# Projecting the first two weight chunks abreast in a hybrid decoder block

## The reference, cut to what matters

```
h = rmsnorm(x, norm_g)                 # x: 1 x 512 x 1024, float32
proj = jnp.einsum('bsd,de->bse', h, w_in)
(lru_u, lru_z, ...) = jnp.split(proj, ...)
xc = conv_b + sum(u_pad[:, k:k + seq] * conv_w[k] for k in range(4))   # lru_u, causal width 4
r = sigmoid(xc @ wa + ba);  i = sigmoid(xc @ wx + bx)                  # per block of 64 channels
```

## Time and profile before

| what | us |
|---|---|
| median of three runs | 414.31 |
| the profiled execution, its own time | 414.59 |
| its span in the profile | 412.8 |
| TensorE busy with matmuls | 405.2 |
| VectorE busy | 283.8 |
| ScalarE busy | 253.0 |

### The profile page before, as it was taken

The page is one execution under the profiler, slowest core; times in us unless marked ns, Lnnn a source line. Parts: engine busy times, 40 slices in busy tenths (PEclk is TensorE's granted clock), DMA queues, the critical chain, the costliest instruction groups (busy, mean ns, idle before and its releaser), DMA issues.

```text
span 412.8 us, 6605 instructions
## 1 busy us (share of the span) xinstructions
PE 405.2 (98%) x2226; PEld 323.4 (78%) x2226; DVE 283.8 (69%) x619; ACT 253.0 (61%) x505; POOL 61.7 (15%) x122
## 2 busy tenths in 40 slices
PE   7999999999999999999999999999899999999996
PEld 5776788889888766666788988988766788888885
DVE  3767759958798876775789677798876599422205
ACT  5946996776475887886168787682887384312200
POOL 3000000000000666565000000000665000000000
PEclk9999999999999999999999999999999999999999
DMA  8922532956512000000327862885500326631005
GB/s 267 358 93 90 168 102 58 238 150 186 148 52 102 2 2 1 2 1 2 103 64 173 220 208 65 237 218 141 134 29 2 102 82 272 207 104 51 2 0 203
DMA packets 17217, 47.85 MB, mean 116 GB/s; under 512 B 2568, under 2 KB 2824, under 8 KB 16928
## 3 DMA queue, kind: packets, MB, share of 16 engines
q1 hardware_dynamic: 16752, 46.85, 37.8%
q10 hardware_dynamic: 432, 0.58, 0.5%
HBM read 32.17 MB, written 2.10 MB: 83 GB/s over the span
## 4 chain that ended last, share of the span: by engine, by line
PE 89%; DVE 5%; DMA 2%; issue 1%; ACT 1%; POOL 0%; SPq 0%; DVEq 0%; ACTq 0%
PE bank L1513 13%; PE bank L1515 13%; PE bank L1514 12%; PE bank L1703 7%; PE bank L1682 6%; PE bank L1800 5%; PE bank L1799 5%; PE bank L1798 5%; PE bank L1672 4%; PE bank L1673 3%; PE bank L1480 3%; PE bank L1481 3%; PE bank L1482 3%; DMA x_raw<-in_xT 2%; DVE y_out L1456 1%
## 5 line engine op out<-in xcount | busy, mean ns | idle before, releaser
L1513 PE MATMUL bank<-xh,wh 128*128 128x512 f32 x240 | 95.3, 397 | 0.0
L1515 PE MATMUL bank<-xh,wl 128*128 128x512 f32 x240 | 93.7, 391 | 0.0
L1514 PE MATMUL bank<-xl,wh 128*128 128x512 f32 x240 | 93.5, 390 | 0.0
L1045 DVE TENSOR_TENSOR wl<-raw,wh 128x1024 fp32r<-128x1024 f32 (+1 forms) x50 | 59.8, 1203 | 31.0 <-ACT wh L643 31.0
L643 ACT ACTIVATE wh<-raw 128x1024 fp32r<-128x1024 f32 (+1 forms) x50 | 51.5, 1037 | 31.4 <-PE bank L1800 28.4
L1281 DVE CUSTOM_DVE_ANT_0 bank<-bank,mask_row 128x256 f32<-128x256 f32 (+3 forms) x96 | 46.7, 498 | 14.2 <-PE bank L1673 14.0
L1513 PEld LDWEIGHTS bank<-xh,wh 128*128 128x128 f32 x240 | 45.1, 188 | 12.3 <-issue 2.8
L1515 PEld LDWEIGHTS bank<-xh,wl 128*128 128x128 f32 x240 | 45.1, 188 | 9.8
L1514 PEld LDWEIGHTS bank<-xl,wh 128*128 128x128 f32 x240 | 45.1, 188 | 8.8
L620 POOL TENSOR_SCALAR probs<-probs,rcp,gates 128x384 f32<-128x384 f32 (+3 forms) x44 | 26.5, 613 | 132.2 <-DVE rcp L1303 132.1
L1798 PE MATMUL bank<-wh,yh 128*128 128x512 f32 x96 | 37.3, 389 | 0.0
(11 more groups left out here) (268 smaller groups left out, 752.2 us busy)
## 6 DMA issues: line engine op xcount, KB each, us to landing
raw<-in_w_in SPq DMA_DIRECT2D x35, 512.0 KB, 3.6
raw<-in_w_out SPq DMA_DIRECT2D x12, 512.0 KB, 3.3
x_raw<-in_xT SPq DMA_DIRECT2D x8, 256.0 KB, 6.7
q_fox<-parts_fox SPq DMA_DIRECT2D x16, 128.0 KB, 2.4
k_fox<-parts_fox SPq DMA_DIRECT2D x8, 256.0 KB, 3.0
x_res<-in_x_tok SPq DMA_DIRECT2D x1, 2048.0 KB, 7.9
out_y<-y_out SPq DMA_DIRECT2D x8, 256.0 KB, 2.1
raw<-in_w_in SPq DMA_DIRECT2D x3, 384.0 KB, 5.0
```

The lines of the kernel that those rows point to most:

```text
L1045: dve.tensor_tensor(wl[:, c % HL, cols], raw[:, c % RAW, cols], wh[:, c % HL, cols].bitcast(F32), ALU.subtract).then_inc(wl_ready, 1)
L1513: pe.matmul(dst, hi, xh[:, k, :], start=(k == 0), stop=False)
L1514: pe.matmul(dst, hi, xl[:, k, :], start=False, stop=False)
L1515: mm = pe.matmul(dst, lo, xh[:, k, :], start=False, stop=(k == KT - 1))
```

## The change

Chunk 0 and chunk 1 are both brought in halves by ScalarE's queue, in the order first half of 0, first half of 1, second half of 0, second half of 1; SyncE no longer issues chunk 1. TensorE multiplies slices 0 to 3 of chunk 0 and then of chunk 1, then slices 4 to 7 of chunk 0 and of chunk 1. ScalarE and VectorE split both chunks in halves, among the slices of x. One square moves from ScalarE to VectorE, `x_sums` goes from chunk 1's slice 4 to its slice 5, and `spread_rstd` from chunk 1's slice 7 to chunk 2's slice 1.

```diff
@@ -93,7 +93,8 @@
 OUT_ORDER = (2, 1, 0, 3)
 Q_SLOT = {1: N_IN - 2, 2: N_IN - 1}
 STACK_LAG = 6
-ACT_SQUARES, VECTOR_SQUARES = (0, 1, 2, 3, 4, 5), (6, 7)
+ACT_SQUARES, VECTOR_SQUARES = (0, 1, 2, 3, 4), (5, 6, 7)
+SUMS_AT, SPREAD_AT = 5, 1
 X_PARTS = KT
 QUARTER = P // NT
 WARM_UP = 8
@@ -212,7 +213,8 @@
         const_loaded, chan_loaded = sem("const_loaded"), sem("chan_loaded")
         lru_w_loaded, cmp_w_loaded = sem("lru_w_loaded"), sem("cmp_w_loaded")
         raw_loaded = [sem(f"raw_loaded{i}") for i in range(RAW)]
-        half_loaded, wh_half, wl_half = sem("half_loaded"), sem("wh_half"), sem("wl_half")
+        half_loaded = [sem("half_loaded0"), sem("half_loaded1")]
+        wh_half, wl_half = sem("wh_half"), sem("wl_half")
         wh_ready, wl_ready, w_used = sem("wh_ready"), sem("wl_ready"), sem("w_used")
         xh_ready, xl_ready, x_sq = sem("xh_ready"), sem("xl_ready"), sem("x_sq")
         x_sq_act, sel_set, zeros_ready = sem("x_sq_act"), sem("sel_set"), sem("zeros_ready")
@@ -540,7 +542,6 @@
             for i in range(X_PARTS):
                 part = slice(i * KT // X_PARTS, (i + 1) * KT // X_PARTS)
                 sp.dma_start(x_raw[:, part, :], xT[:, part, :]).then_inc(x_loaded[i], 16)
-            load_w(1)
             load_w(2)
             sp.dma_start(cst[:, :], const).then_inc(const_loaded, 16)
             load_w(3)
@@ -847,8 +848,10 @@
                         split(FOX_END - 1 + AHEAD)
 
             act.dma_start(chn[:, :], chan).then_inc(chan_loaded, 16)
-            act.dma_start(raw[:, 0, 0:HALF], w_in[0][:, 0:HALF]).then_inc(half_loaded, 16)
-            act.dma_start(raw[:, 0, HALF:D], w_in[0][:, HALF:D]).then_inc(raw_loaded[0], 16)
+            for c in range(2):
+                act.dma_start(raw[:, c, 0:HALF], w_in[c][:, 0:HALF]).then_inc(half_loaded[c], 16)
+            for c in range(2):
+                act.dma_start(raw[:, c, HALF:D], w_in[c][:, HALF:D]).then_inc(raw_loaded[c], 16)
             act.preload_act_table_set("natural_log_exp_and_others")
             act.wait_ge(chan_loaded, 16)
             act.wait_ge(small_consts, 1)
@@ -857,17 +860,24 @@
                 wait_x(act, k)
                 act.activation(xh[:, k, :], x_raw[:, k, :], ACT.Copy, scale=ch("norm_g", k)).then_inc(xh_ready, 1)
 
+            def high_half(c):
+                act.wait_ge(half_loaded[c], 16)
+                act.activation(wh[:, c, 0:HALF], raw[:, c, 0:HALF], ACT.Copy).then_inc(wh_half, 1)
+            def high_rest(c):
+                act.wait_ge(raw_loaded[c], 16)
+                act.activation(wh[:, c, HALF:D], raw[:, c, HALF:D], ACT.Copy).then_inc(wh_ready, 1)
             high_x(0)
-            high_x(1)
-            act.wait_ge(half_loaded, 16)
-            act.activation(wh[:, 0, 0:HALF], raw[:, 0, 0:HALF], ACT.Copy).then_inc(wh_half, 1)
-            high_x(2)
-            high_x(3)
-            act.wait_ge(raw_loaded[0], 16)
-            act.activation(wh[:, 0, HALF:D], raw[:, 0, HALF:D], ACT.Copy).then_inc(wh_ready, 1)
-            for k in range(KT // 2, KT):
+            high_half(0)
+            for k in range(1, KT // 2):
                 high_x(k)
-            split(1)
+            high_half(1)
+            high_x(4)
+            high_rest(0)
+            for k in range(5, KT):
+                high_x(k)
+            high_rest(1)
             for k in ACT_SQUARES:
                 act.activation(x_square(k), x_raw[:, k, :], ACT.Square).then_inc(x_sq_act, 1)
             split(2)
@@ -1318,22 +1328,29 @@
                                          ALU.mult, ALU.subtract).then_inc(xl_ready, 1)
 
             dve.wait_ge(chan_loaded, 16)
+            def low_half(c):
+                dve.wait_ge(wh_half, c + 1)
+                dve.tensor_tensor(wl[:, c, 0:HALF], raw[:, c, 0:HALF], wh[:, c, 0:HALF].bitcast(F32),
+                                  ALU.subtract).then_inc(wl_half, 1)
+            def low_rest(c):
+                dve.wait_ge(wh_ready, c + 1)
+                dve.tensor_tensor(wl[:, c, HALF:D], raw[:, c, HALF:D], wh[:, c, HALF:D].bitcast(F32),
+                                  ALU.subtract).then_inc(wl_ready, 1)
             low_x(0)
-            wait_x(dve, 1)
-            low_x(1)
-            dve.wait_ge(wh_half, 1)
-            dve.tensor_tensor(wl[:, 0, 0:HALF], raw[:, 0, 0:HALF], wh[:, 0, 0:HALF].bitcast(F32),
-                              ALU.subtract).then_inc(wl_half, 1)
-            for k in (2, 3):
+            low_half(0)
+            for k in range(1, KT // 2):
                 wait_x(dve, k)
                 low_x(k)
-            dve.wait_ge(wh_ready, 1)
-            dve.tensor_tensor(wl[:, 0, HALF:D], raw[:, 0, HALF:D], wh[:, 0, HALF:D].bitcast(F32),
-                              ALU.subtract).then_inc(wl_ready, 1)
-            for k in range(KT // 2, KT):
+            low_half(1)
+            wait_x(dve, 4)
+            low_x(4)
+            low_rest(0)
+            for k in range(5, KT):
                 wait_x(dve, k)
                 low_x(k)
-            split_low(1)
+            low_rest(1)
             for k in VECTOR_SQUARES:
                 dve.tensor_tensor(x_square(k), x_raw[:, k, :], x_raw[:, k, :], ALU.mult).then_inc(x_sq, 1)
             split_low(2)
@@ -1493,14 +1510,15 @@
                     pe.wait_ge(pair_done, HEADS // 2)
                 dst = proj_bank(unit)[:, :]
                 if c == 0:
-                    first_chunk(dst)
-                    return
-                if c == 1:
-                    second_chunk(dst)
+                    wait_bank(pe, proj_units(1))
+                    first_chunks([dst, proj_bank(proj_units(1))[:, :]])
+                if c < 2:
                     return
                 if slices[0] == 0:
                     pe.wait_ge(wl_ready, c + 1)
                 for k in slices:
+                    if c == 2 and k == SPREAD_AT:
+                        spread_rstd()
                     if k == KT // 2 and c == AT["kc", 0]:
                         gates_of(2)
                     if k == KT - 1 and c - 1 in NORMED:
@@ -1516,49 +1534,47 @@
                 if slices[-1] == KT - 1:
                     mm.then_inc(proj_done, 1)
 
-            def first_chunk(dst):
-                hi, lo = ([w[:, 0, k * P:(k + 1) * P] for k in range(KT)] for w in (wh, wl))
+            def first_chunks(dsts):
+                def parts(c, k):
+                    return wh[:, c, k * P:(k + 1) * P], wl[:, c, k * P:(k + 1) * P]
                 pe.wait_ge(wh_half, 1)
-                for k in range(2):
+                for k in range(KT // 2):
+                    hi, lo = parts(0, k)
                     pe.wait_ge(xh_ready, k + 1)
-                    pe.matmul(dst, hi[k], xh[:, k, :], start=(k == 0), stop=False)
-                    pe.wait_ge(xl_ready, k + 1)
-                    pe.matmul(dst, hi[k], xl[:, k, :], start=False, stop=False)
-                pe.wait_ge(wl_half, 1)
-                for k in range(2):
-                    pe.matmul(dst, lo[k], xh[:, k, :], start=False, stop=False)
-                for k in range(2, KT):
-                    pe.wait_ge(xh_ready, k + 1)
-                    if k == KT // 2:
-                        pe.wait_ge(wh_ready, 1)
-                    pe.matmul(dst, hi[k], xh[:, k, :], start=False, stop=False)
-                    if k == KT // 2:
-                        pe.wait_ge(wl_ready, 1)
-                    pe.matmul(dst, lo[k], xh[:, k, :], start=False, stop=False)
-                    pe.wait_ge(xl_ready, k + 1)
-                    mm = pe.matmul(dst, hi[k], xl[:, k, :], start=False, stop=(k == KT - 1))
-                mm.then_inc(proj_done, 1)
-            def second_chunk(dst):
-                hi, lo = ([w[:, 1, k * P:(k + 1) * P] for k in range(KT)] for w in (wh, wl))
-                pe.wait_ge(wh_ready, 2)
-                for k in range(3):
-                    pe.matmul(dst, hi[k], xh[:, k, :], start=(k == 0), stop=False)
-                    pe.matmul(dst, hi[k], xl[:, k, :], start=False, stop=False)
-                pe.wait_ge(wl_ready, 2)
-                for k in range(3):
-                    pe.matmul(dst, lo[k], xh[:, k, :], start=False, stop=False)
-                for k in range(3, KT):
-                    if k == 4:
-                        x_sums()
-                    if k == KT - 1:
-                        spread_rstd()
-                    pe.matmul(dst, hi[k], xh[:, k, :], start=False, stop=False)
-                    pe.matmul(dst, hi[k], xl[:, k, :], start=False, stop=False)
-                    mm = pe.matmul(dst, lo[k], xh[:, k, :], start=False, stop=(k == KT - 1))
-                mm.then_inc(proj_done, 1)
+                    pe.matmul(dsts[0], hi, xh[:, k, :], start=(k == 0), stop=False)
+                    if k == 0:
+                        pe.wait_ge(xl_ready, 1)
+                        pe.matmul(dsts[0], hi, xl[:, 0, :], start=False, stop=False)
+                        pe.wait_ge(wl_half, 1)
```

(27 more changed lines are left out.)

## The result

The changed kernel takes 415.09 us (median of 20 runs, 414.81 to 415.43), the kernel before in the same comparison 414.36 us (413.76 to 415.3): a ratio of 1.0015, 95% interval 1.0009 to 1.0022, or 0.4 to 0.9 us slower. The forecast was 415.4; its own range began at 415.1. The medians are 0.73 us apart, less than the 0.83 us that the prediction took as its measure for "slower", so by that measure the outcome is "same", although the interval excludes a ratio of 1. The profiled execution took 414.96 us with a span of 413.2.

What follows compares the result with a forecast made beforehand. TensorE, busy 405.2 of 412.8 us, was taken as the bound. Its own sum was 0.0; a spread 1.4 us later, less air, added 1.13, giving 415.7 for the profiled execution and 415.4 against the median; range 414.1 to 416.3.

Steps and rivals of the forecast that it cites:

- The loop: VectorE and ScalarE, from spread to fourth convolution, form a closed chain without air; gates 3 start 1.13 us late.
- Rival 2: The chain has air: VectorE and ScalarE take up the 1.4 us before the fourth convolution; 414.1 us, chance 0.16.
- Rival 1: Front fed better, x not pushed back, no stalls at slices 1 to 3; shift 1.05, 415.1 us, chance 0.15.
- Rival 3: ScalarE's four weight pieces come ahead of x slices 3 to 7; slice 3 lands at 10.7, 416.3 us, chance 0.09.
- TensorE's own sum: TensorE's gains and stalls up to chunk 2, spread included: even with before, 0.0 us, bounds -0.4 to +0.3.
- the shift: Later start of the spread on TensorE: 22.5 instead of 21.12, 1.4 us, bounds 1.05 and 1.4.
- my lower bound of 1.05: Smallest shift of the spread: sums at 17.36 straight behind the squares, then 12 matmuls; gives 0.78 us.
- shift less 0.28 of air: At gates 3: air of 0.34 us less a hand-over of 0.06 absorbs part of the shift; delay 1.13 us.
- The push back of x: At the start, weight pieces on ScalarE's queue delay x: slice 3 at 9.4 instead of 8.7, slice 7 at 12.8.
- The late spread: Spread behind more matmuls in chunk 2 starts 1.4 us later, making TensorE 1.13 us late at gates 3.
- The transfers: At the start, x and weights land in pairs, 0.68 us per slice; the last x slice at 12.8 instead of 11.5.
- Nothing for ScalarE's two added issues: ScalarE's start: two issues of about 0.45 us each end the table load at 4.35, hidden before the 4.80 copy.

Runs made afterwards that it cites:

- abreast alone: Changed kernel with squares (six on ScalarE, two on VectorE), `x_sums` and `spread_rstd` placed as before the change; 415.07 us, ratio 1.0018.
- and squares first: `a_rest_last` with both engines' squares ahead of the second half of chunk 1, TensorE's wait for that half behind the sums; 414.38 us, ratio 0.9999.
- a_sums_spread: Changed kernel with `x_sums` at chunk 1's slice 4 and `spread_rstd` at its slice 7, transfers as changed; 414.93 us, ratio 1.0011.
- a_spread_early: Changed kernel with only `spread_rstd` put back into chunk 1, ahead of its slice 7; 414.94 us, ratio 1.0015.
- b_spread_late: Kernel before with only `spread_rstd` moved from chunk 1's slice 7 to chunk 2's slice 1; 415.24 us, ratio 1.0023.
- a_rest_last: `a_sums_spread` with the second half of chunk 1 issued by SyncE behind the last slice of x; 414.59 us, ratio 1.0005.

## Why the prediction was right, and which of its steps were not

The marks in one table, from the traces (us; "last square" is its end):

| kernel | last square | sums | spread | gates 3 | ratio |
|---|---|---|---|---|---|
| before, first trace | 16.92 | 17.02 | 21.12 | 43.12 | |
| before, second trace | 16.38 | 16.47 | 20.57 | 42.57 | 0.9999 |
| changed | 16.86 | 17.13 | 21.87 | 43.49 | 1.0015 |
| spread early | 17.07 | 17.34 | 21.44 | 43.47 | 1.0015 |
| abreast alone | 17.28 | 17.53 | 21.62 | 43.62 | 1.0018 |
| before, transfers alone | 17.41 | 17.50 | 21.60 | 43.63 | 1.0018 |
| before, spread late | 16.63 | 16.72 | 22.16 | 43.77 | 1.0023 |
| sums and spread as before | 17.16 | 17.30 | 21.40 | 43.39 | 1.0011 |
| and second half last | 16.82 | 16.97 | 21.07 | 43.08 | 1.0005 |
| and squares first | 16.67 | 16.99 | 21.10 | 43.11 | 0.9999 |

Two constants stand out. With the spread in chunk 1 it starts 4.1 us after the sums in every row: it follows the root (in "spread early" TensorE waits 0.57 us for it). Gates 3 then come 22.0 us after the spread; that is TensorE's own way, without a stall. With the spread in chunk 2 gates 3 come 21.6 us after it in both rows: that is the closed loop. So the end hangs on two things: when the sums start, and whether the spread follows the root or stands behind more matmuls.

**The loop: right.** The lateness of the spread went through four convolutions undiminished (0.75 at the spread's start, 0.64 and 0.65 at the first and the last convolution, against the first trace; the spread ran 1.05 us instead of 1.16, having no pause ahead of it) and ended in a stall ahead of gates 3, released by VectorE. It takes place in the kernel before too, with the late spread alone. Rival 2, air in the chain, is out. Rival 1 said 415.1, which is the time that was measured, but for another reason: it wanted a front without stalls. TensorE's first twelve products took 10.89 - 7.05 = 3.84 us where twelve at 0.23 take 2.8, so about 1.0 us of stalls was there, as the forecast had it, and x was pushed back. The number would have pointed to rival 1; the marks don't. Rival 3 is out too: slice 3 was copied at 8.92. The second, smaller stop in ScalarE's list, which the prediction left out because it would be hidden, was shown when the first was removed.

**TensorE's own sum: mis-sized.** I called it even, with a first matmul at 7.41, sums at 17.7 and the spread at 22.5; it measured 7.05, 17.13 and 21.87, and at the first gates TensorE was 0.69 us ahead of the first trace, outside my bound of -0.4. Most of the miss is that the landings were laid out from one execution: the first half of the weights was copied at 6.37, not 6.74, and x slice 3, whose products are the last to wait, at 8.92, not 9.40. So the shift was 0.75 against the first trace of before, below my lower bound of 1.05, and the profile moved by 0.37 only. That bound was none: it rested on VectorE's squares ending at 17.26, which hung on the same landings (they ended at 16.86). Beside the second trace of before TensorE is 0.14 ahead at the first gates (27.77 and 27.91), close to even, the shift is 1.30 and the delay 0.92. The truth lies between: the mean of the two traces gives a shift of about 1.0 and a delay of about 0.65 (an estimate), the medians a delay of 0.73. So the forecast's rule, shift less 0.28 of air, holds to within 0.1, and its shift of 1.4 and delay of 1.13 were too large by 0.4. The time came within 0.3 us of the forecast because the whole effect is this small; the delay is a third shorter than forecast.

**The push back of x: seen, and its price not followed to the end.** The slices of x pushed back by chunk 1's weights went into my schedule as stalls of TensorE's first matmuls and as later squares; the transfers alone move both, and the sums from 16.47 to 17.50. I set the earlier start, -0.38, against these stalls as a gain of the change; the second trace of before has most of it (7.27). In the changed kernel itself the sums don't wait for the squares. TensorE's last product ahead of them is this:

```profile
16.81 0.39 PE L1576 MATMUL bank<-xl,wh 128*128 128x512 f32 x1
```

The next was due at about 17.04, the last square had ended at 16.86. TensorE has 39 products ahead of the sums instead of 36, as the sums went from slice 4 to slice 5, and that is 0.7 us of the way to 17.13. Put back to slice 4 they gain nothing (`a_sums_spread` 414.93, `a_spread_early` 414.94): TensorE then waits 0.49 us for VectorE's last square. The squares and TensorE's own way stand close behind each other, and moving one meets the other.

**The late spread: not the whole price.** I held it for the whole price. Put back, it saved nothing that was measured: in the changed kernel, sums at 17.13 would give a spread at 21.23 and gates 3 at 43.2, so the late spread adds 0.26 to the late sums' 0.66 (17.13 less 16.47) in these two traces. It adds so little because the sums stand a slice later too: the spread is 4.74 us behind them, 0.6 beyond the root, where in `b_spread_late` it is 5.44. That split is worked out from the constants above, with an early trace of before; the medians, within 0.15 us of each other with and without it, don't resolve it. So the mechanism of the forecast is in the changed kernel, but nearly the same delay came without it, in `a_spread_early`.

**The transfers: as laid out, a little sooner.** x and weights landed in pairs, 0.3 us apart at 7.6 and 7.9. In the changed kernel's profile the last slice of x landed at 12.4, against 11.5; 12.8 had been laid out. The Trainium skill's rule on the two queue rows ("DMA: Bandwidth & Descriptors", "Queues, rings and completion order") gave the right direction, and the pairs agree with it. (Where the prediction says there that otherwise "the second rival would hold", the condition is that of rival 1.) The price had to come from the traces.

**Nothing for ScalarE's two added issues: a thin cover.** I took 0.45 us each; the last two issues took 1.51 together, and the table load moved from 2.14 to 3.69. It ended at 4.97 instead of 4.35, and the first copy started right behind it, at 4.98, without a wait for `chn`. The cover of 0.45 us was used up; the first copy stands at 4.80 and 4.71 in the two traces of before, so this cost at most 0.2 to 0.3 us, ahead of a wait of 0.67 us for the weights.

What stays open: how the delay of the sums divides between TensorE's waits for x, the later squares and the extra split instructions, whether `a_rest_last` differs from before at all (its interval includes 1), and why executions of one kernel differ by 0.5 us in their first landings.

## What to carry to other kernels

Look behind a stage for the first operation from which a closed loop of other engines starts (here the spread of one scale factor): its moment is handed on to the end once the air is used up, and an engine that is 98% busy can hand on a delay that it doesn't show. Before bringing one operand earlier on full queues, ask what is moved back by it and what hangs on that, here the products of the late slices and eight squares. And when the effect is of the size by which the first landings vary, take a second trace of the kernel before ahead of adding up tenths, and look where each traced execution lies among the others.

## What the runs showed of the hardware

GpSimd's squares beside VectorE's splits, which read two tensors, lengthened a split from 0.68 us to as much as 1.52 us. By the ratios the two kernels with them are 1.7 and 2.7 us slower than the kernel before; of the first, about 1.2 us (1.0040 less 1.0011, an estimate) are due to the squares on GpSimd, the rest it shares with `a_sums_spread`. The Trainium skill names this contention ("GPSIMD Engine Reference", "Specifications": shared SBUF interfaces, in contention with VectorE instructions that have two SBUF inputs); the trace agrees. In the changed kernel I had expected no more of it than a smaller gain; it was a loss.
